# Half of the first modulation loads moved beside the first two projection units

## The chip, the cores and the metric

The kernel runs on one core of a Trainium2 chip. The time is the device time of one execution in microseconds (us), and the question is by how much an edit of the kernel's opening, with three small reorderings further on, changes it. TensorE (PE in the profile) multiplies, VectorE (DVE), ScalarE (ACT) and GpSimd (POOL) work on elements, SyncE (SP) issues the transfers.

## The reference

Two layers of a transformer with adaptive normalisation work on 512 latent rows and 256 context rows of width 1024, all in float32. What matters here is how a layer opens:

```python
mod_lat = jnp.split((silu_c @ w_mod[l] + b_mod[l])[:, None, :], N_MOD, axis=-1)
mod_ctx = jnp.split((silu_cc @ w_mod[l] + b_mod[l])[None, None, :], N_MOD, axis=-1)
a_lat = modulate(x, norm1_g[l], mod_lat[0], mod_lat[1])   # rms_norm(x) * (1 + scale) + shift
a_ctx = modulate(h, norm1_g[l], mod_ctx[0], mod_ctx[1])
m_lat, m_ctx = token_mixers(a_lat, a_ctx, w_in[l], w_out[l], ...)
x = x + mod_lat[2] * m_lat
x = x + mod_lat[5] * sq_relu_mlp(modulate(x, norm2_g[l], mod_lat[3], mod_lat[4]), w_ff1[l], w_ff2[l])
```

So nothing can enter the first projection (`w_in`) before the shift and the scale of its rows of weights are known. Each is a product of two conditioning vectors (latent and context) with 1024x1024 of `w_mod`, 4 MB for each of shift and scale.

## The kernel before, in words

**Layout.** Activations lie transposed: 8 blocks (k = 0 to 7) of 128 model columns on the partitions, 768 rows (512 latent, then 256 context) along them. Every float32 operand of a large product is split in a rounded high part and a rest (`Ahi`, `Alo`; `Whi`, `Wlo`), and three products of 128x128 by 512 are summed.

**Units.** Weights come in units of 512 KB into two buffers `raw`. ScalarE rounds a unit to `Whi` (`hi_static`, L759), GpSimd subtracts to get `Wlo` (`low_part`, `low_parts`, L592 and L596). Units 0 to 3 of the first projection hold k = 0,1; 2,3; 4,5; 6,7. `first_unit` (products at L1884) does unit 0 in 36 products; the others are at L1923, also 36 each.

**Normalisation.** For each k VectorE multiplies X by the gain `gs` and by the row's inverse root, which TensorE has spread over the partitions into the PSUM banks ps6 (latent) and ps7 (context) (`norm_full`, L1239); ScalarE adds the shift and rounds to `Ahi` (`norm_hi`, L809); the rest `Alo` is made by VectorE for even k (`norm_low`, L1227) and by GpSimd for odd k (`norm`, L620).

**Modulation in the opening.** 16 loads of 512 KB fill six buffers `modst` in turn. Chunks 0 and 1 are the shifts of k = 0 to 3 and 4 to 7, chunks 2 and 3 their scales. An even load (a scale) goes to VectorE: `start(i)` is four instructions of 128x512 (L1175, L1177) that multiply a slab with the two conditioning columns and add it up in `macc`; after four of them TensorE transposes the sum (`mod_sums`, L1736) and VectorE reduces it (`mod_reduce`, L1204). An odd load (a shift) goes to TensorE: `first_mod(i)` (L1830) holds the two columns of `csil` as weights and streams 512 columns of the slab, twice; ScalarE copies the resulting 2x512 row (`row_copy`, L865), TensorE turns it (`turn_row`), VectorE adds the bias (`shifts`, L1319). X is transposed by TensorE (`x_turn`, L1736), copied and squared by ScalarE (L851, L857). `keep_clock_early` (L1817) is idle work for TensorE. All of this is before the first product at L1884.

**Order.** Each engine has its own list in program order, written out by hand. A wait stops what is behind it on its engine. SyncE issues all loads; a buffer is refilled when the counter of its reader has passed (`mod_first` for VectorE, `mod_pe` for TensorE, `lo_done` for weight units).

**Two later places that the edit touches.** After the retention steps, attention begins: `query_lo` (L1501) makes the low part of queries on VectorE, `attention(s)` takes the maximum of scores (L1560), ScalarE the exponent (L1013), and TensorE waits in attention steps 3 and 4 for the low part of retention's output (`rT_lo`, L1534). Before the feed-forward, VectorE works through late modulation units (`late(i)`), the context's second normalisation (`norm(2)`), and the squared-ReLU steps `hidden(k)` (L1600, L1602); TensorE does one tile of `w_ff1` for each k = 0 to 3 (L2188), with `spread(2)` and a `mod_sums` between them.

## Time and profile before

| what | us |
|---|---|
| median of 3 runs | 1585.25 (1582.49 to 1585.59) |
| profiled execution, its own time | 1586.34 |
| span of its trace | 1584.6 |
| first product of unit 0 | 44.8 |
| first product of unit 2 | 61.6 |

The profiled execution is 1.74 us longer than its span, and 1.09 us above the median. All times of stages are counted from the start of the span. The page gives the busy time of each engine, the chain of work that ended last, and the costliest groups of instructions; the timeline and the windows of the trace show the opening and the two later places.

### The profile page before, as it was taken

The page shows a single profiled execution, that of the slowest core. Times are in us where ns is not written, and L with a number is a line of the kernel's source. Part 1 is how long each engine was busy: PE and PEld are TensorE (multiplying, and loading weights), DVE is VectorE, ACT ScalarE, POOL GpSimd, SP SyncE. Part 2 cuts the span into 40 slices and gives each one's busy share as a digit, 9 for nine tenths or more (in the row PEclk, how much of TensorE's full clock was granted, in tenths as well). Part 3 has the DMA queues.
Part 4 walks back from the last instruction along what each step waited for, and adds up shares of the span by engine and source line. Part 5 has one row for each costly group of instructions (what it writes and reads, how often), then busy time and mean ns, then how long its engine had stood idle before and what let it go on. Part 6 is the DMA issues. An engine that isn't in the chain of part 4 may idle for free.

```text
span 1584.6 us, 22771 instructions
## 1 busy us (share of the span) xinstructions
PE 1556.3 (98%) x8718; PEld 1337.5 (84%) x8718; DVE 920.8 (58%) x1464; ACT 592.7 (37%) x982; POOL 641.2 (40%) x350
## 2 busy tenths in 40 slices
PE   6999999999999999999999999999999999999999
PEld 2888898989788888888888998888997888888887
DVE  5977988766764756444453668697644433233332
ACT  4632367743422121212212244435753422233332
POOL 0535478932433332322322464336104444444443
PEclk9999999999999999999999999999999999999999
DMA  9443203034234444254343433221102333333332
GB/s 325 126 142 105 67 18 107 28 95 119 71 107 130 124 133 130 84 159 130 110 133 107 128 125 107 67 80 41 41 1 80 91 95 93 94 104 93 93 103 97
DMA packets 169473, 161.73 MB, mean 102 GB/s; under 512 B 6548, under 2 KB 133928, under 8 KB 169384
## 3 DMA queue, kind: packets, MB, share of 16 engines
q1 hardware_dynamic: 169384, 160.48, 33.3%
q8 instruction: 63, 1.03, 0.3%
q14 instruction: 26, 0.21, 0.0%
HBM read 158.37 MB, written 2.10 MB: 101 GB/s over the span
## 4 chain that ended last, share of the span: by engine, by line
PE 91%; DVE 3%; ACT 2%; issue 1%; DMA 1%; POOL 0%; SPq 0%; ACTq 0%; POOLq 0%
PE psA L2188 31%; PE psB L2188 30%; PE psA L1923 6%; PE psB L1923 6%; PE ps L2158 4%; PE psS L1923 4%; PE psS L1736 2%; PE ps L1736 1%; DMA modst<-in_w_mod_dram 1%; PE psS L2079 1%; PE psA L2133 1%; PE psB L2133 1%; PE psB L2134 1%; PE psS L1756 1%; PE psA L2134 1%
## 5 line engine op out<-in xcount | busy, mean ns | idle before, releaser
L592 POOL TENSOR_TENSOR Wlo<-raw,Whi 128x1024 fp32r<-128x1024 f32 x156 | 380.8, 2442 | 733.0 <-ACT Whi L759 723.4
L759 ACT ACTIVATE Whi<-raw 128x1024 fp32r<-128x1024 f32 x181 | 191.7, 1059 | 685.1 <-PE psB L2188 351.3
L1347 DVE SCALAR_TENSOR_TENSOR X<-psB,modT,X 128x256 f32<-128x256 f32 (+1 forms) x104 | 67.3, 666 | 129.7 <-PE psB L2188 129.5
L1347 DVE SCALAR_TENSOR_TENSOR X<-psA,modT,X 128x256 f32<-128x256 f32 (+1 forms) x104 | 67.0, 663 | 90.0 <-PE psA L2188 89.9
L1177 DVE SCALAR_TENSOR_TENSOR macc<-modraw,csil,macc 128x512 f32<-128x512 f32 x126 | 111.6, 945 | 1.4 <-DMA modraw<-in_w_mod_dram 1.3
L1602 DVE TENSOR_TENSOR Hlo<-Ab,Hhi 128x512 fp32r<-128x512 f32 (+2 forms) x68 | 72.6, 1067 | 54.2 <-ACT Hhi L1050 54.2
L1600 DVE TENSOR_TENSOR Ab<-psA,Tb 128x512 f32<-128x512 f32 (+2 forms) x34 | 26.7, 785 | 128.6 <-ACT Tb L1042 128.5
L2188 PE MATMUL psA<-Ahi,Whi 128*128 128x512 f32 (+1 forms) x416 | 90.2, 362 | 2.7 <-DVE Ab L1600 2.7
L2188 PE MATMUL psB<-Ahi,Whi 128*128 128x512 f32 (+1 forms) x424 | 89.4, 357 | 0.0
L2188 PE MATMUL psB<-Ahi,Wlo 128*128 128x512 f32 (+1 forms) x424 | 88.9, 356 | 0.0
L2188 PE MATMUL psB<-Alo,Whi 128*128 128x512 f32 (+1 forms) x424 | 88.9, 356 | 0.0
L2188 PE MATMUL psA<-Alo,Whi 128*128 128x512 f32 (+1 forms) x416 | 87.8, 355 | 0.0
L2188 PE MATMUL psA<-Ahi,Wlo 128*128 128x512 f32 (+1 forms) x416 | 87.8, 355 | 0.0
L2158 PE MATMUL ps<-Pk,PTs 128*128 128x64 f32 x640 | 82.4, 273 | 1.7 <-DVE Alo L1534 1.3
L2188 PEld LDWEIGHTS psA<-Ahi,Whi 128*128 128x128 f32 x416 | 71.0, 192 | 14.5 <-issue 2.9
L2188 PE MATMUL psA<-Hhi,Whi 128*128 128x512 f32 (+1 forms) x368 | 82.9, 357 | 0.0
L2188 PE MATMUL psB<-Hhi,Whi 128*128 128x512 f32 (+1 forms) x368 | 82.8, 357 | 0.1
L1600 DVE TENSOR_TENSOR Ab<-psB,Tb 128x512 f32<-128x512 f32 (+2 forms) x34 | 26.7, 784 | 96.5 <-ACT Tb L1042 96.5
L2188 PE MATMUL psB<-Hhi,Wlo 128*128 128x512 f32 (+1 forms) x368 | 82.2, 356 | 0.0
L2188 PE MATMUL psA<-Hlo,Whi 128*128 128x512 f32 (+1 forms) x368 | 82.1, 355 | 0.0
L2188 PE MATMUL psB<-Hlo,Whi 128*128 128x512 f32 (+1 forms) x368 | 82.0, 355 | 0.0
L2188 PE MATMUL psA<-Hhi,Wlo 128*128 128x512 f32 (+1 forms) x368 | 82.0, 355 | 0.0
(383 smaller groups left out, 3385.6 us busy)
## 6 DMA issues: line engine op xcount, KB each, us to landing
raw<-in_w_ff_dram SPq DMA_DIRECT2D x135, 512.0 KB, 4.0
modraw<-in_w_mod_dram SPq DMA_DIRECT2D x72, 512.0 KB, 4.2
raw<-in_w_in_dram SPq DMA_DIRECT2D x36, 512.0 KB, 3.7
modst<-in_w_mod_dram SPq DMA_DIRECT2D x16, 512.0 KB, 7.3
raw<-in_w_out_dram SPq DMA_DIRECT2D x16, 512.0 KB, 3.7
modat<-in_w_mod_dram SPq DMA_DIRECT2D x8, 512.0 KB, 4.5
macc<-in_w_ff_dram SPq DMA_DIRECT2D x5, 512.0 KB, 3.5
Xin<-in_x_dram SPq DMA_DIRECT2D x8, 256.0 KB, 8.0
```

The lines of the kernel that those rows point to most:

```text
L592: nc.gpsimd.tensor_tensor(Wlo[:, s, :], raw[:, s, :], Whi[:, s, :], ALU.subtract).then_inc(S["lo_done"], 1)
L759: nc.scalar.activation(whis[slot], raws[slot], ACT.Copy).then_inc(S["hi_done"], 1)
L1177: ins = V.scalar_tensor_tensor(out=acc[:, s, :], in0=src[:, kk * MCH:(kk + 1) * MCH], scalar=col, in1=acc[:, s, :], op0=ALU.mult, op1=ALU.add)
L1347: last = V.scalar_tensor_tensor(out=X[:, m, c0:c1], in0=pair[p][:, c0:c1], scalar=modT[:, l, 8 * chunk + m, s:s + 1], in1=X[:, m, c0:c1], ...
L1600: V.tensor_tensor(Ab[:, k % 2, c0:c1], pair[k % 2][:, at + c0:at + c1], Tb[:, k % 2, c0:c1], ALU.mult).then_inc(S["h_full"], 1)
L1602: V.tensor_tensor(Hlo[:, hpar, k, c0:c1], Ab[:, k % 2, c0:c1], Hhi[:, hpar, k, c0:c1], ALU.subtract).then_inc(S["h_lo"], 1)
L1736: return nc.tensor.transpose(out, in_, ident[0:n, 0:n])
L1923: return mm(tokbank[t][:, 0:w], (Ahi, Alo)[x][:, k, t * P:(t + 1) * P], (Whi, Wlo)[y][:, uu % 2, cs], start=first, stop=fin)
L2133: mm(out, q, hi_keys, start=True, stop=False)
L2134: last = mm(out, q, lo_keys, start=False, stop=True)
L2158: last = mm((ps6, ps7)[b % 2][:, h * HD:(h + 1) * HD], PTs[:, it % 2, i * P:(i + 1) * P], Pk[:, kt, P + (h // 4) * HD:P + (h // 4 + 1) * H ...
L2188: last = mm(dst[:, c0:c1], weights[w][:, off:off + P], x[:, i, c0:c1], start=(opens and kind == 0 and i == 0), stop=(closes and kind == 2 ...
```

## The change

The 16 modulation loads are no longer all finished before the first projection. Two of them, then all of X, six more, and the first two weight units are issued first; the other eight follow. Loads 0 to 7 give chunks 2 and 0 (scale and shift of k = 0 to 3), enough for units 0 and 1. Loads 8 to 15 are worked on later: TensorE's four (`first_mod(4)` to `(7)`) stand inside and behind `first_unit`, VectorE's four (`start(4)` to `(7)`) stand between and behind its normalisations of k = 0 to 3, and the sum over them (`first_sums(3)`) stands in the middle of unit 1.

A shift is now computed with the slab's 128x128 block as weights and the two columns streaming, straight into PSUM transposed, so the row copy and its turn are gone. A scale is summed over partitions by `first_sums`, a product with a column of ones, in place of eight transposes and two reductions. The context's inverse roots are copied from ps7 to SBUF by ScalarE (`rb_context`), because ps7 now takes the modulation sums.

```diff
@@ SyncE
         for i in range(16):
-            first_mod(i)
             if i == 2:
                 x_load(0, "xa_in")
-            if i == 4:
                 x_load(1, "xb_in")
-        for u in range(2):
-            w_load(u, u, r2(u), proj_src(0, u), True)
+            if i == 8:
+                for u in range(2):
+                    w_load(u, u, r2(u), proj_src(0, u), True)
+            first_mod(i)
@@ GpSimd
-                norm(0)
-                low_parts(2, 10)
+                norm(0, 1, 4)
+                low_part(2)
+                norm(0, 5)
+                low_part(3)
+                low_parts(4, 10)
@@ ScalarE
-        row_copy(0)
-        x_copy(6)
-        x_square(2, 1)
-        x_copy(7)
-        for t in (3, 4, 5):
+        for t in range(2, NT):
             x_square(t, 1)
         norm_root(0)
-        row_copy(1)
+        x_copy(6)
+        x_copy(7)
+        act.wait_ge(S["rb_ready"], 1)
+        nc.scalar.activation(rb_context, ps7[:, 0:CTX], ACT.Copy).then_inc(S["rb_copied"], 1)
         hi_static(0)
...
-                    if k == 1:
-                        hi_static(1)
+                    if k in (1, 3):
+                        hi_static(1 + k // 2)
@@ VectorE
-        for i in range(6):
+        for i in range(4):
             start(i)
-        mod_reduce(0, 2, 0)
-        shifts(0)
-        start(6)
-        norm_root(0)
-        start(7)
+        first_chunk(2, 1)
+        first_chunk(0, 1)
         dve.wait_ge(S["mod_evac"], 2)
         gain(0, 0, 0, 4)
+        norm_root(0)
         dve.wait_ge(S["x_ready"], KT)
         norm_full(0, 0)
-        shifts(1)
         norm_full(0, 1)
-        mod_reduce(0, 3, 1, 2, (psS[:, 0:512], psS[:, 512:1024]))
+        start(4)
+        norm_full(0, 2)
+        norm_full(0, 3)
+        for i in range(5, 8):
+            start(i)
+        first_chunk(1, 2)
+        first_chunk(3, 2)
         dve.wait_ge(S["mod_evac"], 4)
         gain(0, 0, 4, 8)
-        for j in range(2, KT):
+        for j in range(4, KT):
             norm_full(0, j)
...
-                    if l == 0 and s == 2:
-                        query_lo(NT - 1, 1)
...
             attention(1)
+            if l == 0:
+                query_lo(NT - 1, 1)
             retention(TT[l] + 2)
...
-                norm(2)
-                late(7, macc)
+                norm_root(2)
+                late(7, macc, (0,))
+                for j in range(KT):
+                    norm_full(2, j)
+                    if j == 1:
+                        late(7, macc, (1,))
                 for k in range(4):
                     hidden(k, 0, k, LATENT, LAT if k >= 2 else 0)
-                mod_reduce(0, 10, 8)
+                    if k == 2:
+                        mod_reduce(0, 10, 8)
@@ TensorE
             for kk in range(2):
-                last = mm(psS[0:2, 512 * c:512 * c + 512], csil[:, 2 * part + kk, :], modst[:, slot, kk * MCH:(kk + 1) * MCH],
-                          start=(part == 0 and kk == 0), stop=(part == 3 and kk == 1))
+                for t in range(4):
+                    at = FIRST_AT + 8 * c + 2 * t
+                    last = mm(ps7[:, at:at + 2], modst[:, slot, kk * MCH + t * P:kk * MCH + (t + 1) * P], csil[:, 2 * part + kk, :],
+                              start=(part == 0 and kk == 0 and t == 0), stop=(part == 3 and kk == 1 and t == 3))
...
+        def first_sums(c):
+
+            i = 4 * c - 5
+            pe.wait_ge(S["mod_first"], i + 1)
+            pe.wait_ge(S["mod_step"], i * 3 + 3)
+            for t in range(4):
+                for s in range(2):
+                    at = FIRST_AT + 8 * c + 2 * t + s
+                    last = mm(ps7[:, at:at + 1], macc[:, s, t * P:(t + 1) * P], ones[:, :], start=(t == 0 and s == 0), stop=(t == 3 and s == 1))
+            last.then_inc(S["modp_ready"], 1)
...
+        first_mod(0)
+        for m in range(6):
+            x_turn(m)
+        first_mod(1)
+        x_turn(6)
+        first_mod(2)
+        x_turn(7)
+        first_mod(3)
+        first_sums(2)
+        pe.wait_ge(S["mod_evac"], 2)
+        spread(0)
         pe.wait_ge(S["x_ready"], KT)
-        keep_clock_early(4)
...
+        keep_clock_early(8)
@@ TensorE, first_unit and the units behind it
                 pe.wait_ge(S["lo_done"], 1)
                 for t in ts:
                     products(0, 0, 1, t)
+                pe.wait_ge(S["rb_copied"], 1)
+                first_mod(4)
                 pe.wait_ge(S["a_hi"], 2)
                 for t in ts:
                     products(1, 0, 0, t)
                     products(1, 0, 1, t)
+                first_mod(5)
...
                     first_unit()
+                    first_mod(6)
+                    first_mod(7)
...
+                if l == 0 and u == 1:
+                    first_sums(3)
@@ TensorE, before the feed-forward
-                if k == 6:
+                if k == 5:
                     spread(2)
...
-                if l == 0 and k == 3:
+                if l == 0 and k == 2:
                     pe.wait_ge(*a_lo(2, KT - 2))
                     pe.wait_ge(*a_lo(2, KT - 1))
                     pe.wait_ge(S["mod_evac"], 10)
```

The line numbers of the changed kernel differ a little. TensorE's list at the end of the opening, from the last transposes of X to the first product (psA, psB, psS are the accumulators of the projection), was before:

```order
L1736 MATMUL psB<-ident,Xin 128x128 x6
L1736 MATMUL psS<-ident,sqb 128x2 x4
L1736 MATMUL ps6<-ident,macc 128x128 x4
L1736 MATMUL ps7<-ident,macc 128x128 x4
L1830 MATMUL psS<-modst,csil 2x512 x6
L1736 MATMUL ps6<-ident,rstd 128x128 x4
L1736 MATMUL ps7<-ident,rstd 128x128 x2
L1830 MATMUL psS<-modst,csil 2x512 x2
L1817 MATMUL psA<-ident 128x128 x4
```

and is now, from the same place on:

```order
L1747 MATMUL psB<-ident,Xin 128x128 x6
L1843 MATMUL ps7<-csil,modst 128x2 x8
L1855 MATMUL ps7<-ones,macc 128x1 x8
L1747 MATMUL ps6<-ident,rstd 128x128 x4
L1747 MATMUL ps7<-ident,rstd 128x128 x2
L1828 MATMUL psA<-ident 128x128 x8
L1896 MATMUL psA<-Whi,Ahi 128x512
```

The four later `first_mod` have left the opening; two of them now stand in TensorE's list between unit 0 and unit 1, with the sum over VectorE's four behind the first 12 products of unit 1:

```order
L1896 MATMUL psS<-Whi,Alo 128x512 x2
L1843 MATMUL ps7<-csil,modst 128x2 x16
L1938 MATMUL psA<-Whi,Ahi 128x512 x4
L1938 MATMUL psB<-Whi,Ahi 128x512 x4
L1938 MATMUL psS<-Whi,Ahi 128x512 x4
L1855 MATMUL ps7<-ones,macc 128x1 x8
L1938 MATMUL psA<-Whi,Alo 128x512 x2
```

In that last piece nothing but the L1938 and L1896 rows stood before; the products of unit 1 after the first 12 are now behind a wait for VectorE's four units. VectorE's list at the same place (sqb holds the copied inverse roots of the context) is now:

```order
L1225 SCALAR_TENSOR_TENSOR Alo<-Tb,modT,Ahi 128x512
L1173 TENSOR_SCALAR macc<-modst,csil 128x512 x2
L1175 SCALAR_TENSOR_TENSOR macc<-modst,csil,macc 128x512 x2
L1239 SCALAR_TENSOR_TENSOR Ab<-X,gs,sqb 128x256
L1239 SCALAR_TENSOR_TENSOR Ab<-X,gs,ps6 128x512
L1239 SCALAR_TENSOR_TENSOR Ab<-X,gs,sqb 128x256
L1239 SCALAR_TENSOR_TENSOR Ab<-X,gs,ps6 128x512
L1225 SCALAR_TENSOR_TENSOR Alo<-Ab,modT,Ahi 128x256
L1225 SCALAR_TENSOR_TENSOR Alo<-Ab,modT,Ahi 128x512
L1175 SCALAR_TENSOR_TENSOR macc<-modst,csil,macc 128x512 x12
L1320 TENSOR_TENSOR modT<-ps7,bmodT 128x8 x2
```

Sixteen instructions of 128x512 (2 + 2 + 12) now stand between the normalisation of k = 1 and that of k = 4.

## Rows read from the trace of the kernel before

**Rows 1.** The page: shares of the span of the chain that ended last.

```profile
PE 91%; DVE 3%; ACT 2%; issue 1%; DMA 1%; POOL 0%; SPq 0%; ACTq 0%; POOLq 0%
```

**Rows 2.** Timeline, TensorE, units 0 to 2: start us, us, instructions [idle before].

```profile
44.79 0.47 PE L1884 MATMUL psA<-Whi,Ahi 128*128 128x512 f32 x1
...
53.22 1.22 PE L1923 MATMUL psA<-Whi,Ahi 128*128 128x512 f32 x4
...
61.58 1.20 PE L1923 MATMUL psA<-Whi,Ahi 128*128 128x512 f32 x4
```

**Rows 3.** Timeline, VectorE, opening.

```profile
25.12 2.74 DVE L1177 SCALAR_TENSOR_TENSOR macc<-modst,csil,macc 128x512 f32<-128x512 f32 x4 [4.04 <-DMA modst<-in_w_mod_dram]
27.83 0.89 DVE L1175 TENSOR_SCALAR Ab<-modst,csil 128x512 f32<-128x512 f32 x2
...
30.54 2.74 DVE L1177 SCALAR_TENSOR_TENSOR Ab<-modst,csil,Ab 128x512 f32<-128x512 f32 x4 [0.50 <-DMA modst<-in_w_mod_dram]
...
40.23 1.14 DVE L1239 SCALAR_TENSOR_TENSOR Tb<-X,gs,ps 128x256 f32<-128x256 f32 x2
```

**Rows 4.** Timeline, ScalarE, opening.

```profile
16.85 0.81 ACT L851 ACTIVATE X<-psA 128x768 f32<-128x768 f32 x1 [8.93 <-PE psA L1736]
...
18.78 0.62 ACT L857 ACTIVATE sqb<-Xin 128x512 f32<-128x512 f32 x1
19.30 0.19 ACT L857 ACTIVATION_READ_ACCUMULATOR sqb<-Xin 128x1 f32 x1
```

**Rows 5.** Timeline, TensorE: old shift products; transposes; products with a column of ones.

```profile
27.05 1.88 PE L1830 MATMUL psS<-modst,csil 128*2 128x512 f32 x4
37.65 0.84 PE L1736 MATMUL ps<-ident,rstd 128*128 128x128 f32 x6 [0.66 <-DVE rstd L1220]
...
382.80 0.95 PE L1756 MATMUL psS<-ones,sqb 128*128 128x1 f32 x8
383.61 0.72 PE L2188 MATMUL psA<-Ahi,Shi 128*128 128x256 f32 x4
```

**Rows 6.** Timeline, VectorE and GpSimd working at the same time.

```profile
44.24 4.76 POOL L592 TENSOR_TENSOR Wlo<-raw,Whi 128x1024 fp32r<-128x1024 f32 x2 [9.63 <-DVE Alo L1227]
46.70 2.33 DVE L1213 SCALAR_TENSOR_TENSOR gs<-modT,parT 128x8 f32<-128x8 f32 x1
...
52.45 2.18 DVE L1239 SCALAR_TENSOR_TENSOR Tb<-X,gs,ps 128x256 f32<-128x256 f32 x4
53.50 1.86 POOL L620 TENSOR_TENSOR Alo<-Ab,Ahi 128x768 fp32r<-128x768 f32 x1 [2.68 <-ACT Ab L809]
...
62.59 5.37 POOL L592 TENSOR_TENSOR Wlo<-raw,Whi 128x1024 fp32r<-128x1024 f32 x2
62.83 5.67 DVE L1177 SCALAR_TENSOR_TENSOR macc<-modraw,csil,macc 128x512 f32<-128x512 f32 x2
```

**Rows 7.** Timeline and windows (window us, PE busy, granted clock, DMA) where attention begins.

```profile
240.74 4.70 POOL L592 TENSOR_TENSOR Wlo<-raw,Whi 128x1024 fp32r<-128x1024 f32 x2
243.11 2.88 DVE L1501 TENSOR_TENSOR qs<-qT,qs 64x512 fp32r<-64x512 f32 x1
246.78 1.08 PE L2158 MATMUL ps<-Pk,PTs 128*128 128x64 f32 x8 [1.28 <-DVE Alo L1534]
248.00:249.00 1.00, 0.78 (x2) 0.65 1.12 347
254.00:255.00 1.00, 1.00 (x6) 0.50 0.34 129
```

**Rows 8.** Timeline and windows before the feed-forward.

```profile
418.44 5.34 DVE L1177 SCALAR_TENSOR_TENSOR macc<-modraw,csil,macc 128x512 f32<-128x512 f32 x4
429.45 4.51 PE L2188 MATMUL psA<-Ahi,Whi 128*128 128x512 f32 x16 [2.70 <-DVE Ab L1600]
429.00:430.00 1.00, 0.55 (x1) 0.61 0.00 0
432.00:433.00 1.00, 1.00 (x5) 0.69 0.00 0
```

More of the change, by code:

```diff
@@ L613, in rotate, with norm @@
             nc.gpsimd.tensor_tensor(v, tmp[:, 0:256], tmp[:, 256:512], ALU.add).then_inc(out_sem, 1)
-        def norm(n):
+        def norm(n, j0=1, j1=KT):
             c0, c1 = NORMS[n][2]
-            for j in range(1, KT, 2):
+            for j in range(j0, j1, 2):
                 pool.wait_ge(S["a_hi"], 8 * n + j + 1)
```

56 lines of the change are left out of this document (18 added, 38 removed).

## The prediction

> **What bounds the kernel now.** I read the chain of work that ended last first: 91% of the span is TensorE [rows 1]. So an edit counts by what it does to TensorE's start, to its own work, and to its idle time. The timeline comes second. The first product of unit 0 starts at 44.8 us; unit 1 starts at 53.2 and unit 2 at 61.6 [rows 2], and from 44.8 on TensorE hardly stops. The reader is to see two things there: unit 1 took 61.58 - 53.22 = 8.36 us for 36 products, 0.232 us each, and whatever the change does to the opening can be measured by one number, the start of unit 2. Third come the windows with the granted clock. Twice after the opening it falls to half (1.2 for 2.4 GHz), each time behind an idle TensorE: near 248 to 255 us, and near 429.4 to 432.3 us, behind 2.70 us of idleness [rows 7, 8].
>
> **Step 1, the opening until unit 0: gain.** What decides is VectorE's fourth slab. Its load, number 6, has the same bytes ahead of it as before (X and six slabs), so it lands at the same 25.1 us and is worked off 2.74 us later, at 27.9 [rows 3]. Before, four more slabs, two reductions and a turn followed before the first normalisation at 40.2 [rows 3]; now only `first_sums(2)`, the bias, the gain and the spread do. TensorE may be later than 27.9: its `first_mod(3)` stands behind `x_turn(7)`, which needs ScalarE's sixth copy. ScalarE's chain began at 16.85, with the first half of X; one 512 KB slab less is ahead of that now, and four slabs take 30.52 - 25.12 = 5.4 us, 1.35 each [rows 3, 4], so it begins at 15.5. Six copies and eight squares of 0.75 us (0.62 + 0.19 less their overlap) [rows 4] are 10.5 us, 26.0 us. Behind that come one transposition set (0.8), `first_mod(3)` and `first_sums(2)`.
>
> What do the new products cost? No row has two columns streaming over float32 weights of 128x128, but one has one column: eight records in 383.61 - 382.80 = 0.81 us, 0.10 each, and each product makes two records [rows 5]. A new `first_mod` or `first_sums` is eight products, 16 records, 1.65 us. The lower bound is the 0.84 us of six transposes scaled to eight, 1.1; the upper one twice 1.65 at half clock, 3.3. I take 1.65, the row of the same form. The old `first_mod`, four records in 1.88, cost no less [rows 5].
>
> So TensorE is through at 26.0 + 0.8 + 1.65 + 1.65 = 30.1, with waits about 30.8. Bias, gain and reciprocal take 0.9, the spread 0.7, ScalarE's copy of the context's roots 0.4 (half of a copy of 768 columns, 0.81 [rows 4]): the first normalisation starts at about 32.8, 7.4 us earlier. Then `norm_full` 1.1, `norm_hi` 1.1 and `norm_low` 1.1 (each like the 1.14 of [rows 3]) let unit 0 start at 36.1, **8.7 us earlier**.
>
> **Step 2, TensorE's own work behind that: loss.** Four `first_mod` and one `first_sums` move from a time when TensorE waited into one when it is the bound: 5 x 1.65 = **8.25 us**. Up to here the edit is worth about nothing.
>
> **Step 3, the wait in unit 1: loss.** `first_sums(3)` needs VectorE's last four slabs, and behind it on TensorE wait 24 of unit 1's products. TensorE gets there at 36.1 + 36 x 0.232 + 4 x 1.65 + 12 x 0.232 = 53.8. VectorE, from the end of its first `norm_low` at 36.1, has: slab 4, 2 x 0.43 + 2 x 0.68 = 2.2; `norm_full` of k = 2, 3 2.2 and one `norm_low` 1.1; slabs 5 to 7, 12 x 0.685 = 8.2: 13.7 us, 49.8. Alone it would be in time. But GpSimd works then too. At 62.59 it ran two `Wlo` in 5.37 us, and VectorE's two `macc` instructions of the same time took 5.67 us instead of 2 x 0.69: each waited until the GpSimd instruction in progress was over, and the next GpSimd instruction waited for it [rows 6]. An instruction on eight elements took 2.33 us there, while `norm_full`, which reads PSUM, was not slowed by a GpSimd instruction beside it (2.18 for four, as ever) [rows 6]. They take turns, so their times add. GpSimd's work in this stretch is `Wlo` of units 0, 1 and 2, 3 x 2.4, and `Alo` of k = 1 and 3, 2 x 1.86 [rows 6]: 10.9 us. The sum is 36.1 + 13.7 + 10.9 = **60.7 us**, and TensorE idles for 6.9 us. (If unit 2's weights land late, its `Wlo` falls out of the stretch: 58.3.)
>
> The idleness has a second price. Behind 2.70 us of it the clock fell [rows 8], so I let `first_sums(3)` run at half speed: 3.3 us. Then 24 products, 5.5 us: unit 2 starts at 60.7 + 3.3 + 5.5 = 69.5 in place of 61.6. **Opening: +7.9 us.** The chain behind the sum (bias, gain, two `norm_full`, two `norm_hi`, about 5.0 us) is hidden under those 5.5 us; if it is not, what it is over counts. The waits of the loads for `start(4)` delay the issue of unit 2's and 3's weights to about 49 us, which is in time for their use.
>
> The trace has no row for `norm_full` with both tensors in SBUF, which the copied roots make of its context part; GpSimd is idle by my schedule when the four of k = 0 to 3 run, so it costs 0, at most 2.4 us. The Trainium skill (GPSIMD Engine Reference, Specifications) says that the SBUF interface is shared, with contention for VectorE instructions "with two SBUF inputs". By that rule these instructions join those that take turns, which speaks against this edit; if each met one GpSimd instruction the opening would be some 2 us later than by the rows.
>
> **Step 4, `query_lo` before attention: nothing.** It took 2.88 us in place of 0.7, since it was issued at 243.11 just as GpSimd's second `Wlo` began [rows 7]. Now it is issued at about 241.0, 0.3 us behind the start of the first, and ends at 243.8. The wait in front of attention step 4 (1.28 us [rows 7]) goes, but steps 2 and 3 of VectorE come 2.1 us later, and TensorE waits about 1.0 and 1.2 us one and two steps earlier. It reaches step 5 at the same time, about 248.2. The idleness is as large, so I keep the half clock; its price is some 6.8 us at half speed, 3.4 us, the bound of a gain here [rows 7].
>
> **Step 5, late(7) and the sums before the feed-forward: gain.** The four instructions of 5.34 us stood in front of `hidden(0)` at 423.8 and held TensorE until 429.45 [rows 8]. Now two of them fill VectorE's idle time in front of the spread; the other two delay the normalisation by 1.9 us. `hidden(2)` is ready at about 428.2. TensorE gives 1.4 us back waiting for the last `Alo` in front of `mod_sums`, which moved one tile earlier, and is there at about the same time: 1.2 us earlier than 429.45. The long idleness is cut in two, and the half clock until 432.3 goes, 1.4 us [rows 8]: **-2.6 us** (-1.2 if the clock falls all the same).
>
> **The sum.** +7.9 + 0 - 2.6 = +5.3 us. The profiled execution was 1586.34 us, so 1591.6; it lies 1.1 above the median of the runs, so I predict 1590.5. A measurement of this kernel can tell about 0.2%, 3.2 us, from no change: below 1582.1 is faster, above 1588.4 slower.
>
> **The rivals.** (a) VectorE is in time, chance 0.18. If the two engines did not take turns where it counts, `first_sums(3)` would not wait, and unit 2 would start at 53.8 + 1.65 + 5.5 = 60.9: -0.7 in the opening, -2.6 later, 1582, and down to 1578.6 if the clock near 250 us holds. For it: VectorE alone needs only 13.7 us. Against it: every row with both engines on SBUF. It decides at 53.8 us: VectorE must be done by then.
> (b) Half clock in the opening as well, 0.15. The new products stream 2 columns where the old ones streamed 512, and TensorE has gaps between the transposes. If that keeps it at half clock until unit 0, `first_mod(3)`, `first_sums(2)` and the spread cost 1.65 + 1.65 + 0.7 more, everything behind moves 4.0 us: 1594.5. For it: no row shows such products holding the clock. Against: 1.7 us gaps near 22 us did not lower it. In this case the edit also doesn't bring the earlier start that it is made for in full.
> (c) My wait, but the full clock near 250 us, 0.15: 1590.5 - 3.4 = 1587.1.
> (d) A wait of half the size, as with `Wlo` of unit 2 outside the stretch and a quicker opening, 0.10: about 1586.
> The forecast itself (1588.5 to 1592.5) has 0.42.
>
> **How the numbers follow.** Slower: 0.42 + 0.15 = 0.57, less a little of the forecast's edge, 0.56. Within 0.2%: (c), (d) and that edge, 0.26. Faster: (a), 0.18. The range reaches from 1581.5, which takes in most of (a), to 1595, which takes in (b).
>
> **What would show it.** In the trace of the changed kernel: unit 0 starting at 36 (step 1), records of the new products 0.10 us apart (0.21 would be (b)), TensorE idle for about 7 us before the second product with the ones, ended by a `macc` instruction of VectorE (step 3), `macc` instructions of 2.4 us and more beside GpSimd's, unit 2 at 69.5. Near 240 to 256 us the same low windows; near 420 a wait of 1.4 us and no low window behind it. I am wrong if the second product with the ones starts before 55 us.

## The result, and the profile after

The changed kernel took 1594.31 us (median of 4 runs, 1593.96 to 1595.12) against 1585.42 us of the kernel before beside it: a ratio of 1.0061, 95% interval 1.0049 to 1.0074. It is slower by 8.9 us, where 5.3 was forecast. Its profiled execution took 1594.45 us, with a span of 1592.3; before it was 1586.34 and 1584.6. So the two traces differ by 7.7 us of span.

TensorE in the opening of the changed kernel, from the timeline (start, us, engine, line and operation, out<-in, form, records, idle before and what ended it). L1843 are the new products of a shift slab, L1855 the products with the ones, L1896 unit 0, L1938 the later units:

```profile
19.38 0.85 PE L1747 MATMUL psA<-ident,Xin 128*128 128x128 f32 x6 [1.42 <-ACT X L856]
20.72 1.84 PE L1843 MATMUL ps<-csil,modst 128*128 128x2 f32 x16
23.71 1.50 PE L1747 MATMUL psA<-ident,Xin 128*128 128x128 f32 x6 [1.14 <-ACT X L856]
25.00 3.41 PE L1843 MATMUL ps<-csil,modst 128*128 128x2 f32 x16
...
29.58 3.41 PE L1843 MATMUL ps<-csil,modst 128*128 128x2 f32 x16
32.85 3.55 PE L1855 MATMUL ps<-ones,macc 128*128 128x1 f32 x16
37.26 1.51 PE L1747 MATMUL ps<-ident,rstd 128*128 128x128 f32 x6 [0.85 <-DVE rstd L1218]
...
42.95 0.47 PE L1896 MATMUL psA<-Whi,Ahi 128*128 128x512 f32 x1 [1.34 <-DVE Alo L1225]
...
54.91 1.84 PE L1843 MATMUL ps<-csil,modst 128*128 128x2 f32 x16
58.09 3.58 PE L1843 MATMUL ps<-csil,modst 128*128 128x2 f32 x16 [1.34 <-DMA modst<-in_w_mod_dram]
61.53 2.06 PE L1938 MATMUL psA<-Whi,Ahi 128*128 128x512 f32 x4
...
65.87 1.84 PE L1855 MATMUL ps<-ones,macc 128*128 128x1 f32 x16
...
73.14 1.07 PE L1938 MATMUL psA<-Whi,Ahi 128*128 128x512 f32 x4
...
82.67 0.50 PE L1938 MATMUL psA<-Whi,Ahi 128*128 128x512 f32 x1 [1.21 <-POOL Wlo L598]
```

Set these beside [rows 2]. The first product of unit 3 before was this one:

```profile
69.87 0.39 PE L1923 MATMUL psA<-Whi,Ahi 128*128 128x512 f32 x1
```

Unit 0 starts only 1.84 us earlier than before (42.95 against 44.79). Unit 2 starts 11.56 us later (73.14 against 61.58), unit 3 12.80 later. The same 16 records take 1.84 us at 20.72 and 3.41 us at 25.00. The windows of the same trace (window, its length, busy PE, PEld, DVE, ACT and POOL, then granted clock, DMA share, GB/s) say why:

```profile
23.00:24.00 1.00, 0.29 (x2) 0.30 (x3) 1.00 (x2) 1.00 (x2) 0.00 (x0) 0.90 1.06 389
24.00:25.00 1.00, 1.00 (x7) 1.00 (x5) 1.00 (x3) 0.97 (x3) 0.00 (x0) 0.50 1.05 385
...
39.00:40.00 1.00, 1.00 (x6) 1.00 (x6) 0.67 (x2) 1.00 (x2) 0.00 (x0) 0.50 0.00 0
...
58.00:59.00 1.00, 0.91 (x5) 0.91 (x5) 1.00 (x3) 0.00 (x0) 0.00 (x0) 0.50 0.57 151
```

The clock was at half (1.2 for 2.4 GHz) from 23.8 to 40.9 us, although TensorE was busy all the way from 25 to 36, and again from 57.9 to 64.8. VectorE, GpSimd and SyncE's queue in the same stretch (L1173 and L1175 are the scale slabs, L457 the loads of slabs):

```profile
18.76 8.16 DVE L1175 SCALAR_TENSOR_TENSOR macc<-modst,csil,macc 128x512 f32<-128x512 f32 x12 [8.68 <-DMA modst<-in_w_mod_dram]
36.45 0.24 DVE L1320 TENSOR_TENSOR modT<-ps,bmodT 128x8 f32<-128x8 f32 x2 [9.52 <-PE ps L1855]
...
42.73 3.03 DVE L1173 TENSOR_SCALAR macc<-modst,csil 128x512 f32<-128x512 f32 x2
45.68 5.11 DVE L1175 SCALAR_TENSOR_TENSOR macc<-modst,csil,macc 128x512 f32<-128x512 f32 x2
...
54.10 9.58 DVE L1175 SCALAR_TENSOR_TENSOR macc<-modst,csil,macc 128x512 f32<-128x512 f32 x12
67.74 0.24 DVE L1320 TENSOR_TENSOR modT<-ps,bmodT 128x8 f32<-128x8 f32 x2 [4.06 <-PE ps L1855]
```

```profile
42.98 5.03 POOL L594 TENSOR_TENSOR Wlo<-raw,Whi 128x1024 fp32r<-128x1024 f32 x2 [13.96 <-DVE Alo L1225]
47.96 2.28 POOL L622 TENSOR_TENSOR Alo<-Tb,Ahi 128x768 fp32r<-128x768 f32 x1
```

```profile
28.44 23.27 SPq L457 DMA_DIRECT2D modst<-in_w_mod_dram  x5
...
56.84 1.44 SPq L403 DMA_DIRECT2D raw<-in_w_in_dram  x2
```

VectorE waited 9.5 us for TensorE's sums (5.67 us in e4 below, where the slabs ran at full clock). Its fifth slab (`start(4)`) then took 42.73 to 50.72, 8.0 us, beside two `Wlo` and one `Alo` of GpSimd. The last of these five loads, the one for TensorE's last slab, is issued only at the end of that row, at about 51.7, because it stands in the queue behind the load whose buffer `start(4)` frees. That is the 1.34 us wait at 58.09. The wait that I had placed at the second product with the ones did not occur: VectorE, done at 63.7, waited 4.06 us for TensorE.

The two later places, timeline and one window:

```profile
257.41 1.07 PE L2175 MATMUL ps<-Pk,PTs 128*128 128x64 f32 x8 [0.87 <-DVE Alo L1540]
```

```profile
431.00:432.00 1.00, 0.42 (x2) 0.00 (x0) 0.28 (x1) 1.00 (x3) 0.36 (x1) 1.00 0.00 0
```

```profile
432.47 1.07 PE L1747 MATMUL ps<-ident,macc 128*128 128x128 f32 x8 [1.05 <-issue]
...
438.94 3.03 PE L2205 MATMUL psA<-Ahi,Whi 128*128 128x512 f32 x16
```

Of 1.28 us at the attention wait [rows 7] 0.87 are left. In front of the feed-forward the 2.70 us wait and the half clock of [rows 8] are gone, with a 1.05 us wait and full clock in their place.

How far behind is each trace at a given instruction? I took the same instruction of TensorE in each trace and subtracted the start in the first trace of the kernel before. The table has the changed kernel first, then runs that the next section describes.

| kernel | unit 0 (44.8) | unit 2 (61.6) | unit 3 (69.9) | ahead of attention (236.2) | 255.0 | 323.1 | behind the feed-forward's start (433.8) | 1228.4 |
|---|---|---|---|---|---|---|---|---|
| changed | -1.8 | +11.6 | +12.8 | +13.0 | +10.9 | +11.0 | +8.0 | +7.7 |
| changed, second trace | -1.5 | +11.3 | +13.2 | +13.4 | +9.7 | +9.9 | +7.0 | +6.7 |
| e15, opening alone | -3.7 | +9.0 | +10.2 | +10.4 | +7.6 | +8.4 | +8.3 | +8.0 |
| e16, opening and feed-forward edits | -3.9 | +9.3 | +10.6 | +10.7 | +7.9 | +9.0 | +6.0 | +5.8 |
| e4, gaps filled | -5.7 | +6.4 | +8.0 | +8.2 | +6.1 | +6.9 | +3.9 | +3.5 |
| e9, filled with narrow products | +5.6 | +18.6 | +18.7 | +18.9 | +16.8 | +17.6 | +14.6 | +14.4 |
| e1, old opening, later edits | -0.6 | -0.6 | -0.6 | -0.6 | -4.4 | -2.4 | -5.3 | -4.3 |
| e14, old opening, feed-forward edits | -0.8 | -0.8 | -0.8 | -0.8 | -3.6 | -1.9 | -4.8 | -4.8 |
| before, second trace | +0.3 | +0.2 | +0.2 | +0.3 | +0.3 | +0.8 | -0.7 | -0.1 |

The table also shows its own limit. Kernels with the same opening differ by 2.3 us at unit 0, and at 255.0 and 433.8 it depends on whether the clock fell in that trace. Differences below some 2 us between single traces are not evidence; where an instruction waits, and what ends that wait, is.

### The profile page after: what moved, and what is told of

Read it like the earlier page. It is cut to its first block, busy times and chain, and to the rows that moved or that the text cites. A ratio compares the mean times of both kernels' runs of the same rounds, so it can differ in the third digit from the quotient of the medians.

```text
span 1592.3 us, 22946 instructions
## 1 busy us (share of the span) xinstructions
PE 1563.6 (98%) x8810; PEld 1359.9 (85%) x8810; DVE 927.7 (58%) x1460; ACT 592.3 (37%) x981; POOL 641.5 (40%) x350
## 3 DMA queue, kind: packets, MB, share of 16 engines
q8 instruction: 64, 1.05, 0.3%
## 4 chain that ended last, share of the span: by engine, by line
PE 92%; DVE 3%; ACT 2%; issue 1%; DMA 1%; POOL 1%; SPq 0%; POOLq 0%; ACTq 0%; DVEq 0%
PE psB L2205 31%; PE psA L2205 31%; PE psA L1938 5%; PE psB L1938 5%; PE ps L2175 4%; PE psS L1938 4%; PE psS L1747 2%; PE ps L1747 2%; PE psS L2096 1%; PE psA L2150 1%; PE psB L2150 1%; PE ps L1843 1%; PE psS L1767 1%; PE psB L2151 1%; PE psA L2151 1%
## 5 line engine op out<-in xcount | busy, mean ns | idle before, releaser
L594 POOL TENSOR_TENSOR Wlo<-raw,Whi 128x1024 fp32r<-128x1024 f32 x154 | 376.2, 2444 | 730.3 <-ACT Whi L764 716.3
L1175 DVE SCALAR_TENSOR_TENSOR macc<-modraw,csil,macc 128x512 f32<-128x512 f32 x126 | 114.0, 962 | 0.1
L2205 PEld LDWEIGHTS psB<-Ahi,Wlo 128*128 128x128 f32 x424 | 71.6, 189 | 11.6
L2205 PEld LDWEIGHTS psB<-Alo,Whi 128*128 128x128 f32 x424 | 71.6, 189 | 11.5
```

The source lines that it names most:

```text
L594: nc.gpsimd.tensor_tensor(Wlo[:, s, :], raw[:, s, :], Whi[:, s, :], ALU.subtract).then_inc(S["lo_done"], 1)
L1175: ins = V.scalar_tensor_tensor(out=acc[:, s, :], in0=src[:, kk * MCH:(kk + 1) * MCH], scalar=col, in1=acc[:, s, :], op0=ALU.mult, op1=ALU.add)
L2205: last = mm(dst[:, c0:c1], weights[w][:, off:off + P], x[:, i, c0:c1], start=(opens and kind == 0 and i == 0), stop=(closes and kind == 2 ...
```

## The experiments

Two theories to start with. **T1**: the half clock in the opening and in unit 1 (from TensorE's gaps, I thought first, or from the narrow products themselves) and behind it a late VectorE and a late load make the opening's loss. Its rival is that the clock changes little, because VectorE and the loads set unit 2's start anyway. **T2**: the later edits gain as forecast, whatever the opening does. Its rival is that they only trade one wait for another, or gain by the chance of the clock.

**e4: wide products in TensorE's gaps.**

```diff
+        def fill(n):
+            for i in range(n):
+                mm(psS[:, 0:P], ident[:, :], ident[:, :], start=True, stop=True)
         first_mod(0)
         for m in range(6):
+            if m == 4:
+                fill(10)
             x_turn(m)
         first_mod(1)
+        fill(8)
         x_turn(6)
```

> The changed kernel with 18 products of the identity (128 columns each, into a bank that nothing reads yet) in the two gaps in which TensorE waits for ScalarE's copies of the input, ten ahead of the fifth group of transposes and eight behind the second slab's products. Theory (TensorE's gaps from 17.9 to 23.7 us let the granted clock fall at 23.9, and the narrow products then do not bring it back until 40.4): clock 1.00 from 20 to 40 us, first_sums(2) ends near 30.5 instead of 36.4, unit 0 starts near 36.6 instead of 42.95, all behind it shifts by as much; ratio to before 1.0021, 6.4 us under the changed kernel. Rival 1 (products of 2 columns pull the clock down whatever stands beside them): clock 0.50 as in the changed kernel, time within 2 us of it, ratio 1.006 to 1.007. Rival 2 (the opening is not what sets unit 2's start, VectorE's slabs or the loads are): unit 0 early but unit 2 at 71 us or later, ratio 1.005.

Measured: 1590.24 us, ratio 1.0031 (1.0021 to 1.0041), about 4 us under the changed kernel. TensorE's timeline in this run:

```profile
18.54 2.62 PE L1873 MATMUL psS<-ident 128*128 128x128 f32 x20
...
28.92 1.85 PE L1843 MATMUL ps<-csil,modst 128*128 128x2 f32 x16
...
33.40 1.51 PE L1747 MATMUL ps<-ident,rstd 128*128 128x128 f32 x6 [0.85 <-DVE rstd L1218]
...
39.10 0.77 PE L1904 MATMUL psA<-Whi,Ahi 128*128 128x512 f32 x1 [0.77 <-DVE Alo L1225]
```

The slabs run at full clock (1.85 us for 16 records), and unit 0 starts 3.9 us earlier. Of the 6.4 us only 4 came, because the filling itself stands on the path: the transposes of `x_turn(6)` start at 25.87 in place of 23.71, 2.2 us later. The clock still fell, at 32.6 us, behind two narrow groups in a row and during a wait, and the spread ran at half speed as in the changed kernel. The clock's part in the loss is shown; whether gap or narrowness lowers it is not.

**e9: the same gaps filled with narrow products.** The edit is that of e4 with `mm(psS[:, 0:2], ident[:, :], csil[:, 0, :], ...)`, 13 and 10 of them.

> As the run that fills TensorE's two gaps of the opening, but the filling products have 2 columns instead of 128 (13 and 10 of them, for about the same time), so that TensorE has no gap between 18 and 26 us and yet only the transposes are wide. Theory (it is narrow products, not idleness, that let the granted clock fall): clock down near 24 us and 0.50 until about 40 as in the changed kernel, unit 0 at 42 to 43, ratio to before 1.006. Rival (idle gaps alone let it fall): clock 1.00 to 33 us as with the wide filling, unit 0 at 39.1, ratio 1.003.

Measured: 1601.38 us, ratio 1.0105 (1.0090 to 1.0121): 7 us worse than the changed kernel and 11 worse than e4. TensorE's timeline and one window:

```profile
18.69 3.21 PE L1873 MATMUL psS<-csil,ident 128*128 128x2 f32 x26
...
26.83 4.41 PE L1873 MATMUL psS<-csil,ident 128*128 128x2 f32 x20
...
50.38 0.47 PE L1904 MATMUL psA<-Whi,Ahi 128*128 128x512 f32 x1 [0.78 <-DVE Alo L1225]
```

```profile
22.00:24.00 2.00, 2.00 (x15) 2.00 (x14) 2.00 (x4) 1.94 (x6) 0.00 (x0) 0.66 1.05 386
```

TensorE had no gap from 18.7 to 43 us, and yet the clock fell at 22.6 and stayed at half until 49.9. Two kernels that differ in the width of the filling (18 products of 128 columns, 23 of 2) are 11 us apart. So here it is not the gaps alone: filled with narrow products they lost the clock all the same. Single traces scatter, but not by this much. In the eleven traces of the new opening without wide filling the clock fell between 22.6 and 26.5 us, in the two with it (e4, and e13 below) at 32.6 and 30.4. The size of the loss was missed (1.006 expected, 1.0105 measured), because the filling itself ran at half speed on the path: `x_turn(6)` starts at 31.10, 7.4 us later than in the changed kernel, as unit 0 does.

**e5: the last two opening loads exchanged.**

```diff
-        for i in range(16):
+        for i in [*range(14), 15, 14]:
```

> The changed kernel with the last two of the sixteen opening loads exchanged in SyncE's order: TensorE's last slab no longer stands behind the one whose slot VectorE's fifth slab frees at 50.7 us, and is asked for when TensorE's own fifth slab is done (about 49). Theory (the wait of 1.3 us at the last slab and the half clock behind it, 3.3 us more, come from that order): first_mod(7) starts at 56.7 without a wait and at full clock, unit 1's high products run at 1.00; then first_sums(3) waits for VectorE, done at 63.7, so that of the 4.6 us only about 2 are left: unit 2 at 71.1 instead of 73.14, ratio to before 1.0049. Rival (the load's time is set by the DMA queues and not by when it is asked for): the wait stays, unit 2 at 73, ratio 1.006.

Measured: 1592.59 us, ratio 1.0049 (1.0036 to 1.0063). TensorE's timeline and a window:

```profile
53.48 3.97 PE L1843 MATMUL ps<-csil,modst 128*128 128x2 f32 x32
57.30 2.05 PE L1938 MATMUL psA<-Whi,Ahi 128*128 128x512 f32 x4
```

```profile
56.00:57.00 1.00, 1.00 (x9) 1.00 (x9) 1.00 (x3) 0.00 (x0) 0.00 (x0) 0.80 0.61 140
```

The wait for the load is gone, as expected. The clock is not held: it fell at 56.6 during 32 narrow records with no wait ahead of them. That part of the expectation was wrong, and it is what made me look at narrowness. The ratio came out as expected all the same, in part by luck: TensorE, slow at half clock, reached the sums at 62.57, when VectorE was just done (62.3), and unit 0 started 1.4 us earlier than in the changed kernel's trace, with the same opening.

**e3: the last slab behind unit 1's high products** (`first_mod(7)` moved from behind `first_mod(6)` to the place ahead of `first_sums(3)`).

> The changed kernel with TensorE's last slab behind unit 1's high products instead of ahead of them. Theory (VectorE's slabs, done at 63.7 us, are the next bound right behind the load): high products of unit 1 from 56.7 to 61.5 at full clock, the last slab to 63.2, first_sums(3) at 63.8, unit 2 near 71.1 instead of 73.14; ratio 1.0049, the same as with the two loads exchanged, since both end at VectorE. Rival (the wait at the slab alone is what costs, VectorE would have been done earlier): unit 2 near 68.5, ratio 1.003.

Measured: 1594.24 us, ratio 1.0066 (1.0052 to 1.0079): no gain. The expectation (1.0049) was missed. TensorE reached the sums early, waited 2.48 us for VectorE's `macc`, and the clock fell behind that wait. The order of loads was the old one, and VectorE was done at 62.2. Now the wait is where the prediction had put it.

**e10: loads exchanged and the slab apart** (`first_mod(7)` between token blocks 3 and 4 of unit 1's high products).

> The changed kernel with the last two opening loads exchanged, and TensorE's last slab between the fourth and the fifth token block of unit 1's high products instead of right behind the slab before it. With the loads exchanged alone, the 32 narrow records from 53.5 to 57.3 us ran without a wait and the clock fell at 56.7. Theory (two narrow slabs back to back lower the clock; one between wide products doesn't): clock 1.00 until unit 1's high products and the slab are done near 59.7. Then first_sums(3) waits for VectorE (done at 62.3), 2.6 us, and that gap halves the clock for the 24 products behind it, as where the slab came behind the high products: unit 2 at 72.8, no better than 70.2 with the loads exchanged alone; ratio 1.0065. Rival (the wait does not lower the clock here): unit 2 at 70.0, ratio 1.005.

Measured: 1594.25 us, ratio 1.0062 (1.0049 to 1.0076). TensorE:

```profile
59.70 1.19 PE L1937 MATMUL psS<-Whi,Ahi 128*128 128x512 f32 x4
63.26 3.57 PE L1855 MATMUL ps<-ones,macc 128*128 128x1 f32 x16 [2.37 <-DVE macc L1175]
66.70 1.20 PE L1937 MATMUL psA<-Whi,Alo 128*128 128x512 f32 x2
```

Both halves came as expected (unit 2, at 74.8, even 2 us later than expected, as the clock stayed at half from 61.9 to 72.1): apart, the narrow slabs leave the clock at 1.00 (the high products run at 1.19 us for four), and then the wait for VectorE takes it all back.

**e11: the same with VectorE's last three slabs on 32 of 512 columns.** This leaves out most of the scales of k = 4 to 7.

> The kernel with the last two loads exchanged and the slab apart, in which VectorE works on 32 of the 512 columns in its last three opening slabs (the second chunk's modulation is incomplete; all transfers, waits and counts stay), so that VectorE is done some 6 us earlier, at about 56. Theory (what is left beyond TensorE's own moved work is VectorE's lateness): first_sums(3) starts at 59.7 without a wait at full clock, unit 2 at 67.0, against 72.8 with all columns; ratio to before about 1.0025 (5.8 us under the run with all columns). Rival (unit 2's weights, whose load VectorE does not set, are the next bound within 2 us): unit 2 not before 69, ratio 1.004.

Measured: 1588.14 us, ratio 1.0028 (1.0016 to 1.0040), 6.1 us under e10:

```profile
60.55 1.84 PE L1856 MATMUL ps<-ones,macc 128*128 128x1 f32 x16
```

No wait and the sums at full clock; the clock fell only behind the narrow sums, from 62.3 to 65.8. VectorE's lateness is shown to be the second bound, worth about 6 us once the load and the clock no longer hide it.

**e19: GpSimd's `Wlo` of units 0 and 1 on 32 of 1024 columns.** This leaves the low weight parts of these two units mostly out.

```diff
-        low_parts(0, 2)
+        for s in range(2):
+            pool.wait_ge(S["hi_done"], s + 1)
+            nc.gpsimd.tensor_tensor(Wlo[:, s, 0:32], raw[:, s, 0:32], Whi[:, s, 0:32], ALU.subtract).then_inc(S["lo_done"], 1)
```

> The changed kernel in which GpSimd forms the low parts of the first two weight blocks for 32 of their 1024 columns (the first units are less exact; waits and counts stay), so that it does not take turns with VectorE's fifth slab. Theory (VectorE is late because of GpSimd): the fifth slab takes about 3 us instead of 8.1, VectorE's last slab ends near 58.8 instead of 63.7, the load behind it is asked for in time, TensorE's last slab starts at 56.7 without a wait; the two narrow slabs back to back still halve the clock for unit 1's high products, unit 2 near 70.2 instead of 73.1; ratio to before 1.0045, 2.6 us under the changed kernel. Rival (the fifth slab is slow by itself, its two first operations from a slot that a load is filling): it still takes 8 us and the time stays at 1.006.

Measured: 1591.25 us, ratio 1.0038 (1.0026 to 1.0051), 2.8 us under the changed kernel measured beside it (e17 below). VectorE's timeline:

```profile
42.96 0.88 DVE L1177 TENSOR_SCALAR macc<-modst,csil 128x512 f32<-128x512 f32 x2
43.75 1.41 DVE L1179 SCALAR_TENSOR_TENSOR macc<-modst,csil,macc 128x512 f32<-128x512 f32 x2
...
46.13 1.41 DVE L1243 SCALAR_TENSOR_TENSOR Ab<-X,gs,sqb 128x256 f32<-128x256 f32 x1
```

The four instructions of the fifth slab take 2.1 us in place of 8.0, and the last load is in time (TensorE has both slabs in one stretch from 55.1 us). So the turns with GpSimd are shown. The clock fell all the same during the 32 narrow records, at 57.8, and unit 2 started at 71.9, not at the expected 70.2. The third line shows one thing more: a normalisation instruction with the roots in SBUF took 1.41 us beside a GpSimd `Alo`, against 0.48 alone.

**e12: loads exchanged, slab apart, and the sums behind the products with the low input.**

```diff
-                if l == 0 and u == 1:
-                    first_sums(3)
                 if not whole:
                     for kk in range(nk):
...
                         for t, w in here:
                             product(t, w, kk, 1, 0)
+                    if l == 0 and u == 1:
+                        first_sums(3)
```

> The changed kernel with the last two opening loads exchanged, TensorE's last slab apart from the one before it, and first_sums(3) behind unit 1's products with the low half of the input instead of ahead of them. With the slab apart and the sums ahead, TensorE waited 2.4 us for VectorE's slabs (done at 63.2) and then ran 24 products at half clock; with VectorE's work made light both were gone and 6.1 us with them. Theory (the wait can be covered: those products need nothing from VectorE's slabs): high products and the slab to 60.8, low-input products to 63.5, sums to 65.2 without a wait and at full clock; unit 2, which needs the fifth and sixth normalised tiles 4 us behind the sums, at about 69.5 against 74.8; ratio to before 1.0029, 5.3 us under 1594.25. Rival (the chain sums, normalisation, high copy then holds unit 2 up instead, and the gap halves the clock for it): unit 2 at 71 to 72, ratio 1.0045.

Measured: 1590.55 us, ratio 1.0043 (1.0030 to 1.0056), 3.7 us under e10; the rival's number.

```profile
69.64 1.15 PE L1937 MATMUL psA<-Whi,Ahi 128*128 128x512 f32 x3 [1.50 <-ACT Tb L814]
70.59 1.91 PE L1937 MATMUL psB<-Whi,Ahi 128*128 128x512 f32 x4
```

The wait for VectorE's sum is covered, and the next one is the chain behind it (sums, gain, normalisation, ScalarE's copy), for which unit 2 waits 0.8 and 1.5 us, with half clock behind.

**e13: the same with the filling of e4 and 10 wide products more around `first_sums(2)`.**

> The same with wide products (identity, 128 columns) filling TensorE's waits in the opening: 10 and 8 of them as in the earlier run, 4 ahead of first_sums(2) and 6 behind it. Theory (clock 1.00 through the whole opening): unit 0 at 39, the gain of the filling, 4.2 us, adds to that of the later sums; ratio to before 1.0003. Rival (as VectorE starts earlier by the filling but TensorE's units too, the chain behind the sums takes half of it back): ratio 1.0017.

Measured: 1592.74 us, ratio 1.0042 (1.0029 to 1.0055): no better than e12, where 4 us less were expected. The clock fell at 30.4 us, behind two slabs with one set of transposes between them, and most of the ten added products then stood on the path at half speed, so unit 0 started at 43.1. In this run the wide products behind the fall brought the clock back only at 40.7.

**e1, e2 and e14: the later edits on the kernel before.** e1 has both, e2 the move of `query_lo`, e14 the edits in front of the feed-forward (the pieces of the diff at `query_lo`, `late`, `spread(2)`, `mod_reduce(0, 10, 8)` and the `k == 2` wait).

> The kernel before with the two later edits alone: the last query part's low half behind the first blocks, and in front of the feed-forward the split last slab, the earlier spread and the earlier sums; the opening stays as before. Aligned by TensorE's instructions, the changed kernel came through these two places 2.1 us and 2.9 us better than the kernel before. Theory (the later edits gain by themselves, independent of the opening): ratio to before 0.9968, 5.0 us less. Rival (the first of the two is luck of the clock near 250 us, which the late opening had moved): about 0.9980, 2.9 us less, with the half clock near 250 us as wide as before. Forecast of the prediction: 2.6 us, ratio 0.9984.

> The kernel before with the query part's move alone. In the kernel with both later edits TensorE was 3.5 us ahead of the kernel before at 259 us and 2.4 us at 323 us, and a further 2.9 us ahead behind the feed-forward's start. Theory (the move gains by shortening the gap that lowers the clock near 248 us): ratio to before 0.9985, 2.4 us. The prediction's value for this step was 0, with a bound of 3.4 us. Rival (the gain at 259 us is given back before the feed-forward, at waits that end with VectorE): ratio 0.9995 or more.

> The kernel before with the edits in front of the feed-forward alone (last slab split around the normalisation, spread one step earlier, sums one hidden step earlier). Theory: TensorE at 433.8 us is 2.9 us ahead of the kernel before and stays so; ratio 0.9982. The prediction's value was 2.6 us. Rival (given back at the next VectorE-bound stretch): under 1 us, ratio 0.9995.

Measured: e1 1581.86 us, 0.9977 (0.9968 to 0.9986); e2 1583.18 us, 0.9991 (0.9982 to 1.0000); e14 1581.85 us, 0.9984 (0.9975 to 0.9993). The feed-forward edits gain some 2.7 us. The query's move gains nothing that could be told from zero. e1 gains less than its expectation (0.9968), and beats both kernels.

**e15, e16, and both kernels again.** e15 is the new opening alone, e16 the new opening with the feed-forward edits.

> The changed kernel with both later edits taken back, so that the new opening stands alone. By TensorE's instructions the changed kernel was 12.9 us behind before the attention and 7.7 behind at the end. Theory (additive): ratio to before 1.0061 plus what the two later edits gave on the old opening (3.6 us measured, 5.0 us by the instructions), 1.0084 to 1.0092. Rival (the half clock near 250 us falls elsewhere with a late opening, so the later edits gave less there): ratio 1.0075 or less.

> The changed kernel with the query part back in its old place, the feed-forward edits kept. Theory (the query move is worth nothing, the clock near 250 us falls or not by chance of the run): ratio as the changed kernel's, 1.0055 to 1.0065, and TensorE 2.9 us less behind at 434 us than at 408. Rival (the query move does count): 1.0075.

> The changed kernel again, for a second trace beside the others of this call. Theory (scatter): ratio 1.005 to 1.0065; where the clock falls in the opening (23.9 us in the first trace, 24 to 26 in others with the same opening) and whether it falls near 260 differ from trace to trace by 1 to 3 us in all. Rival (each kernel's trace is the same every time): clock at half from 23.9 and around 262 again.

> The kernel before again, for a second trace. Theory (the half clock from 248 to 254 us of its first trace is chance): full clock there and some 3 us less in that trace, ratio 1.0 within the interval. Rival: the same half clock again, since it comes from the query part's wait.

Measured: e15 1594.65 us, 1.0061 (1.0048 to 1.0074); e16 1594.19 us, 1.0058 (1.0045 to 1.0071); the changed kernel again 1594.06 us, 1.0059 (1.0046 to 1.0071); the kernel before again 1584.32 us, 0.9993 (0.9984 to 1.0001). So what the edits give does not add up: e15, without the later edits, was expected at 1.0084 to 1.0092 and is as fast as the changed kernel. The same wait of attention in e15, with `query_lo` in its old place, then e15 before the feed-forward, and the kernel before at both places in its second trace:

```profile
257.16 1.08 PE L2168 MATMUL ps<-Pk,PTs 128*128 128x64 f32 x8 [1.28 <-DVE Alo L1538]
...
437.90 4.38 PE L2198 MATMUL psA<-Ahi,Whi 128*128 128x512 f32 x16 [2.70 <-DVE Ab L1604]
```

```profile
247.04 1.08 PE L2158 MATMUL ps<-Pk,PTs 128*128 128x64 f32 x8 [1.30 <-DVE Alo L1534]
...
430.25 3.04 PE L2188 MATMUL psA<-Ahi,Whi 128*128 128x512 f32 x16 [2.70 <-DVE Ab L1600]
```

e15 has the old wait of 1.28 us and full clock behind it; the kernel before has 1.30 us and half clock again (the expectation, full clock, was missed); the changed kernel had 0.87 us and half clock once (259 to 263 us), full clock the second time. In front of the feed-forward the same 2.70 us wait halved the clock in the first trace [rows 8] and not in the second, where 16 records took 3.04 us. So the same wait lowers the clock in one trace and not in another. Over all eighteen traces the feed-forward edits stand out: the four without them (both of the kernel before, e2, e15) have the wait of 2.70 us, and in three the clock fell at its end or within 1 us behind it; in the fourteen with them it never fell there.

T2 is half settled. On the new opening the feed-forward wait goes too: in the table the changed kernel and e16 gain about 3 us between 323.1 and 433.8, and e15 gains nothing there. But the medians differ by only 0.3 to 0.6 us, with intervals of about 2 us on each. **Open:** whether the whole 2.7 us is there on the new opening. The runs' scatter, 5 us from lowest to highest of the changed kernel, is too large for these runs to say.

## Why the prediction was wrong, point by point

The sign was right (slower, held most likely) and the time within the range, at its upper edge. The forecast missed by 3.8 us; two of its terms missed by 6.9 and 3.8, with opposite signs, and that they partly cancel is luck. So is a third part: the opening lost 12.8 us where 7.9 was forecast, and from there to the end of the trace 5.1 came back where 2.6 was forecast. Not all of that is the edits' doing, since e15, without the later two, got 2.2 us back too. (The profiled run lay 0.1 us above its median, not 1.1; that is 1.0 of the 3.8.) The table puts the terms of the opening beside the first trace of the changed kernel, up to unit 3.

| term | forecast | trace |
|---|---|---|
| step 1, start of unit 0 | -8.7 | -1.8 |
| step 2, five narrow groups on TensorE | +8.25 | +8.5 (5 x 1.70, start to start) |
| step 3, wait and half clock in unit 1 | +8.5 | +4.7 (wait 1.3, slab 1.7, high products 1.6) |
| unit 3 waits for its weights | 0 | +1.2 |
| rest | -0.15 | +0.2 |
| opening | +7.9 | +12.8 |

**Step 1 failed, and by the clock.** The forecast took 1.65 us for each group of new products, "the row of the same form", and held the half clock as an upper bound and as rival (b), at 15%. The row was right for full clock: 1.84 us at 20.72, 1.70 from start to start. But every group of the opening from 25.0 us on ran at half. From the 30.8 forecast for the end of `first_sums(2)` to the 36.4 measured, and on to unit 0, 6.9 us were lost. The half clock cost 0.65 and 0.67 on two sets of transposes, 1.57 on each of two slabs, 1.71 on the sums, 0.66 on the spread: 6.8 in all. What else differed from the forecast came to nothing on balance. Rival (b) had the mechanism, with 4.0 us; e4 and e9 show it. What I argued against it ("1.7 us gaps near 22 us did not lower it") compared gaps between wide products with gaps between narrow ones, and rested on one trace: in the second trace of the kernel before a wait of 3.34 us there did lower it, from 23.2 to 26.6 us.

**Step 2 held**: 1.70 us a group against 1.65.

**Step 3 had the resources right and the place wrong.** VectorE needed 63.65 - 42.80 = 20.9 us from the end of its first `norm_low` to the end of its last slab; the forecast had 24.6. The turns with GpSimd made up the difference to the 13.7 us alone. In `start(4)` they cost 5.9 us, beside two `Wlo` and the `Alo` of k = 1. In `start(5)` one instruction took 2.29 us in place of 0.74, beside the `Alo` of k = 3. Unit 2's `Wlo` came behind it all (65.7 us), the case that the prediction had in brackets.

Why was there no wait of 6.9 us at the sums? Not because of step 1, since VectorE began as late as TensorE did. VectorE needed 3.7 us less than forecast, and TensorE took 22.9 us from unit 0 to the sums (42.95 to 65.87) in place of 17.7: the 1.3 us wait for the load, 1.7 on a slab and 1.6 on the high products at half clock, 0.5 of other small parts. Where the load is in time and the clock holds up to the sums, as in e10, the wait is there, with 2.37 us. The wait that came was one that the prediction passed over in one clause: "the waits of the loads for `start(4)`". I had looked at what that does to the weights behind them in SyncE's queue and not at the next slab in it. e5 and e19 show that wait and its cause. The half clock came behind that wait, and not behind one at the sums. The mark of being wrong, the second product with the ones before 55 us, was not hit (65.9).

**"In time for their use" failed by 1.2 us.** The weights of units 2 and 3 were asked for at 56.8 us, not at 49. GpSimd makes unit 3's `Wlo` behind `Alo` of k = 7 in its list, and so behind VectorE's whole late chain; TensorE waits 1.21 us for it at 82.67. A late chain alone does not explain it: in e4 the chain ended 5 us earlier and the wait was 1.57. What differs is one instruction, the next point.

**The copied roots** were priced at 0, at most 2.4 us. In the changed kernel such an instruction beside GpSimd's `Alo` took 2.12 us at 72.67 and in e19 1.41, against 0.47 to 0.48 alone. So the rule of the Trainium skill that was cited there (GPSIMD Engine Reference, Specifications) agrees with the trace. The four of k = 0 to 3 ran with GpSimd idle, as forecast. But the one at 72.67 holds up the chain to unit 3: from its start to the end of unit 3's `Wlo` (79.79 + 2.82) it is 9.9 us. In e5 and e10 the same instruction started level with the `Alo`, took 0.47 and 0.48 us, and unit 3's `Wlo` was through 7.6 us behind its start, with no wait of TensorE's. In the seven traces with a wait of 0.2 us or more for that `Wlo` (the changed kernel twice, e4, e13, e15, e16, e19) the instruction took 2.1 us. So the term of 0 was some 2.4 us on VectorE's and GpSimd's chain, and most likely the whole 1.2 us of TensorE's wait. The edit wasn't undone on its own, so that price is argued from these traces and not tested.

**Step 4 held**: zero forecast; e2 gave 1.4 us, interval 0 to 2.9. The bound "if the clock holds" was real, but not tied to the edit: of the thirteen traces with `query_lo` in its new place the clock fell near there in six, and of the five with it in its old place in two.

**Step 5 held**: 2.6 us forecast, 2.7 measured on the old opening; but 1.4 of the forecast was a half clock which only three of the four traces with the old wait have. On the new opening it is open in the medians.

## What to carry to other kernels

Before moving narrow products (two columns here) into a stretch, ask what they do to the clock. In e5 a run of 32 records lost it with no wait ahead; in e10, with wide products between the slabs, it stayed up until TensorE waited. To size a wait between two engines, count both from a common start: a lateness that both share (some 7 us here) changes nothing in it, and half clock or a late load on the waiting engine hides it. And when a load is made to wait for a reader, check every load behind it in the same queue, the next one first.

## What the runs showed of the hardware that I had not expected

- During 32 narrow records in 3.97 us, with no wait ahead of them, the clock went from 1.00 to 0.50 (e5). It stayed at half for 17.1 us in the opening of the changed kernel, through 10 us of such records and with no gap from 25.0 to 36.4, and for 27 us in e9. In unit 1 of the changed kernel it came back at 64.8, in the wide products that began at 61.5.
- Products of two columns and transposes of 128 both took twice the time at half clock (3.41 for 1.84, 1.51 for 0.85).
- The same wait of 2.70 us halved the clock in one trace of the kernel before, in e2 and in e15, and not in the other trace of the kernel before.
- A VectorE instruction with one tensor and a column of scalars as inputs also takes turns with GpSimd: the two `TENSOR_SCALAR` of the fifth slab took 3.03 us beside `Wlo` and 0.88 beside the shortened one (e19).
